# A hybrid attention layer on one core: weight loads later in SP's order, the block turn's write and return split, squares summed on ScalarE, the last scaling later, projection pieces dealt anew

## The reference

```
h = RMSNorm_pre(x);  P = h @ W_in             (1024 x 1024 by 1024 x 3328)
A: sliding-window attention, 8 query heads on 2 k/v heads of 64, sinks, ALiBi, chunks of 64
B: differential attention, 4 heads, two softmax maps each (q, k of 64; v of 128), ALiBi, causal
   by chunks, in 128-query blocks: attn = p0 - lambda * p1;  o = attn @ v;
   o = RMSNorm over the head's 128 outputs * g * (1 - lambda_init)
each group's output * SiLU(its gate columns of P)
y = concat(A, B) @ W_out;   out = x + RMSNorm_post(y)
```

## Time and profile before

| | |
|---|---|
| median of three runs | 525.46 us (524.62 to 526.19) |
| the profiled execution | 522.7 us |
| its span | 520.9 us |
| PE busy | 489.9 us (94%) |
| DVE, ACT, POOL busy | 305.5 (59%), 223.7 (43%), 112.5 us (22%) |
| mean granted PE clock | 0.978 |
| SP waits for `w_lo` (L661) | 104.6 us in 14 waits |
| SP waits for a landing of turn_store (L712) | 92.5 us in 32 waits |
| DMA queues' share | SP's queue 35.9% |

### The profile page before, as it was taken

How to read it: one execution, slowest core, us unless ns; L and a number is a source line. 1 busy time by engine, 2 the same in 40 slices (tenths; PEclk the granted TensorE clock), 3 DMA queues, 4 the chain that set the end, 5 groups by cost and what they waited for, 6 DMA issues and landing times.

```text
span 520.9 us, 7224 instructions
## 1 busy us (share of the span) xinstructions
PE 489.9 (94%) x2576; PEld 413.3 (79%) x2576; DVE 305.5 (59%) x690; ACT 223.7 (43%) x508; POOL 112.5 (22%) x131
## 2 busy tenths in 40 slices
PE   9999999799897898979999999999999959999995
PEld 9999988688785786868887777788888848888884
DVE  4969834736746568365667677565763286433332
ACT  7943833524424245333466575633431172222311
POOL 1073431402213032112034336221230000000000
PEclk9999999989999899998999999999999979999999
DMA  8820231233581546533450340133323483332222
GB/s 292 279 87 1 81 79 40 60 107 99 165 197 33 135 126 193 133 91 112 151 161 3 81 102 9 39 67 105 114 75 102 98 246 121 107 136 81 82 81 81
DMA packets 81618, 56.69 MB, mean 109 GB/s; under 512 B 35312, under 2 KB 73648, under 8 KB 81584
## 3 DMA queue, kind: packets, MB, share of 16 engines
q1 hardware_dynamic: 79136, 52.05, 35.9%
q10 hardware_dynamic: 2448, 4.20, 2.2%
HBM read 38.94 MB, written 13.65 MB: 101 GB/s over the span
## 4 chain that ended last, share of the span: by engine, by line
PE 72%; DMA 8%; DVE 7%; issue 5%; ACT 4%; SPq 3%; POOL 2%; POOLq 0%; DVEq 0%; ACTq 0%
PE proj L1326 30%; PE scores L1430 15%; PE scores L1263 8%; PE banks L1363 5%; DMA turn_store<-weights 4%; PE scores L1352 4%; DMA weights<-turn_store 2%; PE scores L1388 2%; PE banks L1408 2%; SPq L714 1%; DMA wo_raw<-in_w_out 1%; PE banks L1396 1%; PE banks L1263 1%; PE proj L1263 1%; DVE weights L1134 1%
## 5 line engine op out<-in xcount | busy, mean ns | idle before, releaser
L764 POOL TENSOR_TENSOR w_lo<-w_raw,w_hi 128x256 fp32r<-128x256 f32 x84 | 71.9, 884 | 184.0 <-ACT w_hi L842 184.0
L1326 PE MATMUL proj<-hT_hi,w_hi 128*128 128x512 f32 x336 | 89.5, 399 | 3.2 <-DVE k_stack L1097 3.2
L924 ACT ACTIVATE weights<-weights,small 128x128 f32<-128x128 f32 (+7 forms) x64 | 49.2, 770 | 100.0 <-DVE small L1161 100.0
L1326 PE MATMUL proj<-hT_lo,w_hi 128*128 128x512 f32 x336 | 90.3, 405 | 0.0
L1326 PE MATMUL proj<-hT_hi,w_lo 128*128 128x512 f32 x336 | 90.0, 403 | 0.0
L1326 PEld LDWEIGHTS proj<-hT_hi,w_lo 128*128 128x128 f32 x336 | 62.7, 192 | 13.6 <-issue 0.4
L1326 PEld LDWEIGHTS proj<-hT_lo,w_hi 128*128 128x128 f32 x336 | 62.9, 193 | 12.6 <-issue 0.4
L1326 PEld LDWEIGHTS proj<-hT_hi,w_hi 128*128 128x128 f32 x336 | 60.8, 188 | 15.2 <-DVE k_stack L1097 4.1
L1161 DVE CUSTOM_DVE_ANT_1 weights<-scores,dist_b 128x128 f32<-128x128 f32 (+6 forms) x56 | 36.3, 684 | 34.2 <-PE scores L1352 34.0
L1363 PEld LDWEIGHTS banks<-weights,v_sb 128*128 128x128 f32 x288 | 36.8, 193 | 18.7 <-DMA weights<-turn_store 16.8
L1363 PE MATMUL banks<-weights,v_sb 128*128 128x128 f32 x288 | 38.8, 280 | 13.5 <-DMA weights<-turn_store 13.5
(11 more groups left out here) (123 smaller groups left out, 705.4 us busy)
## 6 DMA issues: line engine op xcount, KB each, us to landing
w_raw<-in_w_in SPq DMA_DIRECT2D x13, 512.0 KB, 4.1
w_raw<-in_w_in SPq DMA_DIRECT2D x16, 256.0 KB, 3.8
x_res<-in_x SPq DMA_DIRECT2D x8, 512.0 KB, 4.4
out<-y_out ACTq DMA_DIRECT2D x14, 256.0 KB, 2.5
x_all<-in_xT SPq DMA_DIRECT2D x6, 512.0 KB, 7.5
k_stack<-k_stack SPq DMA_DIRECT2D x12, 256.0 KB, 3.9
turn_store<-weights SPq DMA_DIRECT2D x4, 512.0 KB, 4.0
weights<-turn_store SPq DMA_DIRECT2D x16, 128.0 KB, 2.5
```

The source lines that it names most:

```text
L764: nc.gpsimd.tensor_tensor(w_lo[:, n % SPLIT, k], w_raw[:, n % RAW, k], w_hi[:, n % SPLIT, k].bitcast(F32), ALU.subtract).then_inc(w_lo_rea ...
L924: nc.scalar.activation(w, w, ACT.Exp, scale=-1.0, bias=min_b[:, 2 * u + m:2 * u + m + 1], accum_out=sum_b[:, 2 * u + m:2 * u + m + 1]).the ...
L1326: last = nc.tensor.matmul(to, w[:, slot, k, :], h[:, k, HALF * half:HALF * half + HALF], start=(p == 0 and k == first), stop=(p == PIECES ...
```

## The change

A step `load` for the weights of unit n + 4 comes behind piece 2 of the second half of unit n. `turn` ends with the write; the return is a step of its own, `b_return`, behind the vector parts of the next slot, so that k's copy falls between the two. Held k is stored just ahead of the last scores of a head. `b_square` makes four activations of 128 x 128 with a sum each, in place, and DVE's reduce goes. The ending has one stage more (`b_root` a slot behind `b_back`), its steps stand ahead of a slot's last pieces for A, and the last `b_finish` goes behind the last piece. `PIECES_BESIDE` and `AFTER_VALUES` are new.

```diff
@@ -85,15 +85,16 @@
 B_UNITS = B_HEADS * TILES
 
 
-PIECES_BESIDE = ([9, 4, 3, 4, 4, 5, 3, 7] + [5, 5, 3, 3, 5, 5, 3, 7] + [5, 5, 3, 4, 3, 5, 3, 6]
-                 + [6, 6, 6, 6, 6, 5, 5, 5]
-                 + [4, 7, 7, 6, 3, 6, 5, 5] + [8, 4, 3, 2])
+PIECES_BESIDE = ([9, 6, 3, 3, 3, 3, 3, 6] + [6, 6, 4, 4, 4, 3, 3, 6] + [6, 6, 4, 4, 4, 4, 4, 5]
+                 + [7, 6, 6, 6, 6, 5, 5, 5]
+                 + [4, 6, 6, 6, 5, 6, 5, 5] + [8, 4, 3, 2])
 
 PIECES_AHEAD = {8: 1, 16: 1, 36: 1, 37: 1}
 MIX_FIRST = {8}
 MORE_AHEAD = {31}
 OUT_EVERY = 2
-AFTER_VALUES = 2
+AFTER_VALUES = 1
+ENDING = [None, "b_back", "b_root", "b_spread_out", "b_spread_in", "b_finish"]
 
 
 def slope_a(h):
@@ -116,6 +117,8 @@
             if half == 0 and p == 0 and n + 2 < NU:
                 steps.append(("split", n + 2))
             steps.append(("project", n, half, p))
+            if half == 1 and p == 2 and n + 2 + RAW < NU:
+                steps.append(("load", n + 2 + RAW))
             if half == 0 and p < LOWS and n + 2 < NU:
                 steps.append(("low", n + 2, p))
             if p < PIECES - 1:
@@ -157,6 +160,17 @@
             ending.append([u // 4, 0])
 
     ending = []
+
+    def end_heads():
+
+        for at_end in ending:
+            f, stage = at_end
+            if 0 < stage < len(ENDING) and ("b_finish" != ENDING[stage] or f < B_UNITS // 4 - 1):
+                steps.append((ENDING[stage], f))
+                if ENDING[stage] == "b_back":
+                    steps.append(("b_square", f))
+            at_end[1] += 1
+
     steps += [("split", 0), ("split", 1)]
     take(FIRST_PIECES)
     vector_parts()
@@ -178,10 +192,17 @@
         turning = turns.get(slot)
         if turning is not None:
             steps.append(("a_transpose", 2 * turning))
+        if kind == "b" and now % TILES == TILES - 1:
+            for later_n, half in held:
+                store(later_n, half)
+            held.clear()
+            vector_parts("store_low")
         scored = (f"{kind}_scores", now) in steps
         if kind and not scored:
             steps.append((f"{kind}_scores", now))
         vector_parts()
+        if last[0] == "b" and last[1] != 3 * TILES:
+            steps.append(("b_return", last[1]))
         if turning is not None:
             alone = 1 + scored
             take(alone)
@@ -199,16 +220,12 @@
             if kind == "a":
                 steps += [("a_exp", 2 * now + 1), ("a_weights", 2 * now), ("a_scale", 2 * now)]
             else:
-                steps += [("b_mix", now), ("b_turn", now)]
+                steps += [("b_mix", now), ("b_turn", now), ("b_return", now)]
             steps.append(("a_values", turning))
             if kind == "a" and now + 1 < STEPS_A:
                 steps += [("a_weights", 2 * now + 1), ("a_scores", now + 1)]
         else:
             if kind == "b":
-                if now % TILES == TILES - 1:
-                    for later_n, half in held:
-                        store(later_n, half)
-                    held.clear()
                 steps.append(("b_exp", now))
             if slot in due:
                 ahead = 1 if kind == "a" else max(1, count - AFTER_VALUES)
@@ -221,29 +238,23 @@
                 steps += [("a_exp", 2 * now), ("a_exp", 2 * now + 1), ("a_weights", 2 * now), ("a_scale", 2 * now)]
         if kind == "a":
             steps.append(("a_scale", 2 * now + 1))
+        if kind == "a":
+            end_heads()
         take(1)
         count -= 1
-        if kind != "a" and slot not in MIX_FIRST:
-            vector_parts("store_low")
-        for at_end in ending:
-            f, stage = at_end
-            steps += [[], [("b_back", f), ("b_square", f), ("b_root", f)], [("b_spread_out", f)],
-                      [("b_spread_in", f)], [("b_finish", f)]][stage]
-            at_end[1] += 1
-        ending = [at_end for at_end in ending if at_end[1] < 5]
+        if kind != "a":
+            if slot not in MIX_FIRST:
+                vector_parts("store_low")
+            end_heads()
         take(max(0, count))
     last = (NU - 1) * 2 * PIECES
     outs = list(range(KT))
     while at < len(pieces):
         take(1)
+        if at == len(pieces):
+            steps.append(("b_finish", B_UNITS // 4 - 1))
         vector_parts()
-        for at_end in ending:
-            f, stage = at_end
-            if at % 4 == 0:
-                steps += [[], [("b_back", f), ("b_square", f), ("b_root", f)], [("b_spread_out", f)],
-                          [("b_spread_in", f)], [("b_finish", f)]][stage]
-                at_end[1] += 1
-        ending = [at_end for at_end in ending if at_end[1] < 5]
+        end_heads()
         if outs and at >= OUT_FROM and at % OUT_EVERY == 0:
             steps.append(("split_out", outs.pop(0)))
         if at == last + PIECES + 1:
@@ -433,7 +444,6 @@
     b_turn_stored = sem("b_turn_stored")
     b_turned = [sem("b_turned0"), sem("b_turned1")]
     b_valued = sem("b_valued")
-    b_summed = sem("b_summed")
     b_floored = sem("b_floored")
     b_meaned = sem("b_meaned")
     b_rooted = sem("b_rooted")
@@ -709,6 +719,12 @@
                 sp.wait_ge(b_blocks_turned, u + 1)
                 sp.dma_start(turn_store[u % 2, :, :, 0:width].rearrange("g p x -> p g x"),
                              by_group(weights_of(u), blocks)).then_inc(b_turn_stored, 16)
+
+            def turn_back(u):
+
+
+                blocks = u % TILES + 1
+                width = GROUP * blocks
                 sp.wait_ge(b_turn_stored, 16 * (u + 1))
                 for g in range(4):
                     sp.dma_start(by_group(weights_of(u)[GROUP * g:GROUP * (g + 1)], blocks),
@@ -716,10 +732,12 @@
                                  ).then_inc(b_turned[u % 2], 16)
 
             for step, *i in SCHEDULE:
-                if step == "low" and i[1] == LOWS - 1 and i[0] + RAW < NU:
-                    load_w(i[0] + RAW)
+                if step == "load":
+                    load_w(*i)
                 elif step == "b_turn":
                     turn(*i)
+                elif step == "b_return":
+                    turn_back(*i)
                 elif step == "b_spread_out":
                     f = i[0]
                     if f:
@@ -930,10 +948,12 @@
                 elif step == "b_square":
                     f = i[0]
                     if f:
-                        act.wait_ge(b_finished, f)
+                        act.wait_ge(b_meaned, f)
                     act.wait_ge(turned_full, turned_count("b_back", f))
-                    nc.scalar.activation(on_b[:, :, :], turned.rearrange("p (u e) -> p u e", e=P),
-                                         ACT.Square).then_inc(turned_read, 1)
+                    for j in range(4):
+                        last = nc.scalar.activation(turned[:, P * j:P * j + P], turned[:, P * j:P * j + P], ACT.Square,
+                                                    accum_out=square_b[:, j:j + 1])
+                    last.then_inc(turned_read, 1)
                 elif step == "a_exp":
                     c = i[0]
                     s = 4 * (c % 4)
@@ -1168,11 +1188,8 @@
                     dve.wait_ge(turned_read, turned_count("b_back", f))
                     if f:
                         dve.wait_ge(b_rooted, f)
-                    nc.vector.tensor_reduce(square_b, on_b[:, :, :], mybir.AxisListType.X,
-                                            ALU.add).then_inc(b_summed, 1)
                     nc.vector.scalar_tensor_tensor(floor_b, sum_0, EPS, sum_0, ALU.mult,
                                                    ALU.mult).then_inc(b_floored, 1)
-                    dve.wait_ge(b_summed, f + 1)
                     dve.wait_ge(b_floored, f + 1)
                     nc.vector.scalar_tensor_tensor(mean_b, square_b, 1.0 / P, floor_b, ALU.mult,
                                                    ALU.add).then_inc(b_meaned, 1)
```

## The result

The changed kernel took 509.82 us, the median of three runs (509.39 to 511.94), against 525.46: a ratio of 0.971 [0.967, 0.976], 15.6 us less. The forecast was 510.0, with 501 to 518 as its range. Measured again beside the experiments it took 508.97 against 522.76, a ratio of 0.974 [0.972, 0.976], 13.8 us less. The profiled executions give 12.9 us (522.7 to 509.8); the kernel before's own was 2.8 us under its median. So the gain is 13 to 15.6 us, and the forecast's 15.2 is at its upper end. That 510 came within 0.2 us of 509.82 is in part luck: on the profiled executions the sum was 2.3 us too high, and it was taken off a median that lay 2.8 above its own profiled execution.

A forecast was written before the change was run, and what follows sets the result against it. PE's work plus its waits for turned weights was taken as the bound: 22.9 us to be had, less 7.0 staying late, 0.2 and 0.5, gives 15.2 off 525.46, so 510 us, range 501 to 518.

The forecast's parts named there:

- The bound: PE, busy 94%: its work plus its waits, mainly for turned weights in differential heads 0 to 2, 17.6 us idle.
- the part on the write and return: Heads' ends: k's copy goes between write and return, early store_low frees the projection's bank; two k_stack waits, 3.2 us, go.
- The sum: Whole kernel: 22.9 - 7.0 - 0.2 - 0.5 = 15.2 us gained, taken off the median 525.46; forecast 510.
- the estimate for the clock: Matmuls behind waits in differential heads 0 to 2 run at a lower granted clock: 5.3 us to be had.
- What stays late: Tight units (0, 1, 3, 7, 9, 12, 15, 22) and scores 16 still wait: 7.0 us together.
- The waits of 265 to 420 us: PE's 1.1 us idle there stays; in the windowed heads a transpose waiting for the longer square loses 0.2 us more.
- Squares: Four activations with an accumulator on ScalarE take 1.6 us against 0.6; DVE loses its reduce and 16.5 us of waits.
- The junction: Before out_project, w_out loads begin 1.2 us nearer the end: 0.5 us lost, ends 2 gained or 2 lost.
- (a): All waits go, since the slacks are larger than thought: 501.5 us, 15%.
- (b): The DMA queue is the bound: some six tight units lose 1.3 us more each, 518 us, 20%.
- (c): The loop of DVE and ACT becomes the bound in slots of three or four pieces: slower, up to 528 us, 5%.
- (d): The change does not do what it says and the waits just move: 524 to 526 us, 5%.

The follow-up runs named there:

- old_squares: The changed kernel with one square activation of 512 columns into `on_b` and DVE's reduce, as before: 514.87 us, 0.985 of the kernel before.
- the deal alone: The kernel before with the new PIECES_BESIDE and AFTER_VALUES = 1, nothing else: 524.62 us, 1.004 of the kernel before.
- early_slabs: The changed kernel with slabs 0 to 2 of w_out loaded behind the last return: 507.4 us, 0.969 of the kernel before.
- old_deal: The changed kernel with the old PIECES_BESIDE and AFTER_VALUES = 2: 520.54 us, 0.996 of the kernel before.
- loads_on_act: The changed kernel with the weight loads of units 4 to 20 issued by ScalarE on its own queue: 505.08 us, 0.967 of the kernel before.

## Why the prediction was right, and where not

**The bound** was read right: PE's waits for the turned weights and the clock lost behind them. What went is there, but for 1.1 us in the windowed heads. One reading was wrong: I called the two waits for `k_stack` waits for k's copy, but they stood before pieces of the projection, for the bank that the store_low frees (the part on the write and return says so itself). The scores waited for the copy for 0.9 us in all.

**The sum** against the profiled executions: the projections' last matmul ended at 419.8 us before and 406.3 after, 13.5 earlier. By the rows: 17.6 idle and 1.1 from 265 to 420 us, plus the 5.3 for the slow clock, less the 10.7 that stay, is 13.3. So the estimate for the clock, read as what is left over, holds within a few tenths. Three terms behind it were off, and the first is the one that matters:

- *What stays late*: 10.7 us (9.1 in the repeat) instead of 7.0. Units 0 (1.07 for 0.8), 9 (0.97 for 1.1) and 15 (0.75 for 1.0) came as worked out. Unit 3 was 2.27 for 1.0, unit 12 1.86 for 0.5: I had 2.1 us and 0.7 to 1.2 for the load in front, and it takes 2.8 (4.96 less 2.12) and 2.2 (4.37 less 2.13). My figure of at most 2.5 came from unit 18's 4.49, the right row; for 12 I took less than it. Unit 7 was 2.34 for 0.8: that was an estimate from the order alone, with no price for its return, which took 5.8 us where I had 3.35 for all that I worked out; at 3.35 it would not have waited. Scores 16 and units 1 and 22, forecast at 1.8 together, did not wait; units 2 and 17, 1.45 together, did.
- *The waits of 265 to 420 us*: I let them stay and added 0.2. They went, 1.1 gained. The largest, 0.65 us at 291.47, was a transpose that waited for the old square in its bank, and no transpose waits in the kernel after. Which part did it (squares, or the ending's new places) was not separated; old_squares shows only that the old square in the new places would cost 3.69 us there. That the old square needs `on_b`, and so b_finish, is in no term of my sum.
- *Squares*: 1.2 us for four (391.80 to 393.0), not 1.6. The row I took, at 391 ns, reads a bias per partition; these groups of the kernel after read nothing of that kind (count, busy us, mean ns, idle before):

```profile
L954 ACT ACTIVATE banks<-banks 128x128 f32<-128x128 f32 x32 | 8.5, 265 | 13.2 <-PE banks L1389 13.2
L954 ACT ACTIVATION_READ_ACCUMULATOR banks<-banks 128x1 f32 x32 | 6.0, 187 | 0.0
...
L1191 DVE SCALAR_TENSOR_TENSOR small<-small 128x4 f32<-128x4 f32 x8 | 1.4, 173 | 2.4 <-ACT banks L954 2.3
```

DVE now waits 2.4 us over eight heads where it waited 16.5, as forecast. The Trainium skill ("ScalarE: Activation LUTs", What ACT_TABLE_LOAD costs) has an activation with immediates at 186 ns + 0.833 ns a column, 93 more for each pointer operand; for 128 columns that gives 293 and 386, near the 265 and 391 here. An estimate by it, four at 293 ns, is 1.2 us, the time measured; the reads of the sums (187 ns each, overlapping in part) are not in it.

**The junction** cost 0.6 us (projections' end to first pass's end: 12.0 before, 12.6 after), for 0.5 forecast, and much by the forecast's parts: the idle ahead of out_project fell from 5.87 to 4.91, and its first pass grew, with three new waits for wo_hi. The chain after shows the load of w_out as the bound, 13.84 us from its last issue:

```profile
394.55 1.42 DMA spread_store<-small
...
396.35 0.55 SPq L682
...
403.13 13.84 DMA wo_raw<-in_w_out
416.99 1.07 ACT wo_hi L904
418.10 7.10 PE scores L1447 x30
```

**The signs I gave.** Idle 6 to 8 us: it was 10.7, and 9.1 in the repeat. No gap over 2 us: there are two, 2.27 and 2.34. Clock 0.99 or more: yes. SP's wait for w_lo all but gone: no, 66.3 us in 7 waits (104.6 in 14 before), since the early loads still wait for it. Writes 3 and 12 in about 4 us, 18's in 2 to 3: 4.96, 4.37, 2.13.

**The rivals.** (a), all waits go, is out. (b), the queue as a bound, is the one half true: the load in front takes 2.2 to 2.8 us where it stands, and taking the loads off SP's queue gave 3.9. But in the kernel after it hit units 3 and 12, and with 0.89 us unit 17 (write to return 4.86, a load and the spread ahead), not six. (c), the loop of DVE and ACT, does not show in the kernel after: no scores wait. In the two kernels with the new deal on the old order it shows, small: 1.8 us in two waits of scores for DVE's minimum. (d) is out for the whole, but true for each half: the deal alone is 1.9 us slower than before and the order alone 2.2 faster.

**What the total hides.** Undone one at a time they cost 11.6 (deal), 6.5 (k early), 5.9 (squares), 4.7 (loads) and 0.8 (split), together 29.5 us, for a change that is worth 13.8 to 15.6. The later last scaling and the ending's new stage were not undone by themselves. My sum priced most of the waits one unit at a time in the final order, and not by the worth of each part; I take that to be why it came near. The prices I then gave to the parts in the expectations (9 to 13 us for the deal alone) were wrong, as they took the waits of k's copy to be fixed in size: with the pieces dealt anew PE was ready for the scores 5.2 us earlier and the copy was issued 2.0 earlier.

## What to carry to other kernels

In a pipeline with little slack, a wait is also cover for what comes next: follow each unit through the final order of every queue, and don't add up the parts. When an instruction is moved off an engine, ask which buffer it frees: here a transpose waits 3.69 us for that buffer in the new order with the old square, against 1.3 us that the old square and reduce take. A bulk load ahead of a small, urgent transfer on the same queue cost that transfer 2 to 4 us here, so give the load a place with nothing tight behind it, or another queue.

## What was not expected of the hardware

- What a wait costs in clock does not follow from its length alone. The sixteen matmuls of unit 7 or 15 took 2.05 us behind 2.34 in the kernel after, but 3.07 behind 1.87 in early_slabs, 2.93 behind 3.63 in old_deal and 3.78 behind 3.25 in loads_on_act. My rule in the sum, that only the long waits cost clock, does not hold wait by wait.
- A spread of 4 floats a partition took 5.79 us behind 1.5 MB on its queue, and the same one 2.07 in the kernel after.
- Two returns of the same size differ: unit 7's took 5.8 us from its first issue to its use in the kernel after (5.72 in the repeat), unit 15's 4.20 (4.40), one of four blocks 3.47. The bytes alone do not give the time; what else does was not found.
